# The first two tiles behind a norm, multiplied before the norm's row is known

## Chip, cores and metric

One core of one Trainium2 chip runs the whole program. The metric is the device time of one execution in microseconds (us), less is better.

## What is computed

The reference is a model of 512 tokens of width 1024: a first block of two layers (each an FFN, a token mix of attentions, another FFN), a final norm, and a later block with four branches and one last FFN. What the change touches is the norm in front of two products:

```python
def rms_norm(x):
    xf = x.astype(jnp.float32)
    return (xf * lax.rsqrt(jnp.mean(xf * xf, -1, keepdims=True) + NORM_EPS)).astype(x.dtype)
...
    h = rms_norm_2(x, norm1_g)          # later block
    z = h @ w_in + b_in
...
    h2 = rms_norm_2(x, norm2_g)         # last FFN
    x = x + jnp.square(jax.nn.relu(h2 @ w_up)) @ w_down
```

The norm of a token is one number per token; the gain is one number per feature. The kernel keeps x transposed (features on partitions, tokens along the free axis), so a token's number stands in a row that is the same on all partitions, and multiplies a product's columns alike whether it is applied before or after the matmul.

## The kernel before

All of x (eight pieces of 128 features by 512 tokens) stays on chip. Each matrix product is made of output tiles of 128 features: eight pieces k, and for each three matmuls (lines 445 to 447), because both operands are split into a high and a low part (`uh` and `ul` for the activations, `wh` and `wl` for the weights). A tile has so 24 matmuls of 128x512.

Weights come in the order of one list, `plan()`. SyncE loads a tile into one of five `raw` buffers; ScalarE rounds it into one of three `wh` buffers (line 943), VectorE takes the remainder (line 1427, `wl`); both do this when their own program reaches `get` for the tile two before it, and ScalarE then waits until TensorE is done with the tile three before it. `fm` handles one tile, `fm_pair` two tiles piece by piece, so that pieces can be used as they are made. ScalarE and VectorE evict the results. Each engine's order is the order of its own function, written out by hand, with semaphores between them.

Results go to eight banks in a ring: `take` gives the next one and waits until what was in it has been evicted (a "free" signal). At line 689 the counter of the ring is set to 4, `second()` makes the ring six banks long from bank 0 on, and its end makes it eight again from bank 0 on.

In front of the later block (stage "s") and of the last FFN (stage "up") the order is: TensorE sums the squares (line 488; passes with one column, against a column of ones), VectorE makes means, GpSimd the power -1/2 (line 2095), VectorE diagonal matrices (line 1465), TensorE turns them into a row on all partitions (line 495), then `apply` for each k: VectorE multiplies x by gain and row (line 1498), ScalarE copies this into `uh` (line 977), VectorE takes the remainder into `ul` (line 1461), and only then TensorE multiplies piece k. In front of the later block there are two norms in a row, the final one and the block's own; their rows are made together, and `final(k)` (ScalarE, line 1228) and GpSimd (line 2166) bring x itself up to date during the first tiles. The last down tiles of stage f21 and the tiles of `wo2`, which stand ahead of the two seams, end with an update of x (lines 1517, 1515); GpSimd and ScalarE square it as it comes.

Behind the row ScalarE evicts the later block's first tiles into `lqk` (line 1237); in the last FFN it applies Relu (line 1004), VectorE squares (line 1538), ScalarE rounds into `fh` (line 1010) and VectorE makes `fl`.

Of the kernel before, what the change touches and what calls it, by code (L numbers as in the profile page):

```python
# [14 lines left out]
def plan():  # L15
# [14 lines left out]
    def ffn(g, u, d, nf, ahead=False):  # L30
        for a, n in chunks(nf, CHUNK_FF):
            for j in range(a, a + n):
                if ahead and j < 4:
                    continue
                if j == 0 and u:
                    pair(g, 0, u, 0)
                elif j < 2 and not u:
                    if j == 0:
                        pair(g, 0, g, 1)
# [66 lines left out]
    for c in range(2, 13):  # L106
        fm("zml", 8, c)
# [136 lines left out]
def program(nc, A, OUT):  # L244
# [66 lines left out]
    with ExitStack() as c:  # L311
# [6 lines left out]
        with ExitStack() as d:  # L318
            lqk = sb(d, "lqk", [128, 8, 512])
# [80 lines left out]
    bank_of = {}  # L400
# [12 lines left out]
    def tensor_engine(pe, TE):  # L413
# [55 lines left out]

        def tm(g, name, nk, w, per, h, l, key):  # L470
# [20 lines left out]
        def row(g, dg):  # L491
# [4 lines left out]
            ins.then_inc(*s_pe.up(("ps", g)))  # L496

# [7 lines left out]
        def ffn(st, first=False):  # L505
# [190 lines left out]


# [213 lines left out]
        o = take(("fs", 0))  # L911
        pe.wait_ge(*s_pool["sq", "s"])
        sums(o, 0, acc)
        pe.wait_ge(*s_pool["sq fin"])
        sums(o, 4, more).then_inc(*s_pe.up(("ps", ("fs", 0))))
        o = take(("fs", 1))
        pe.wait_ge(*s_act["tail", "s"])
        sums(o, 0, tmp[1]).then_inc(*s_pe.up(("ps", ("fs", 1))))
        o = take(("fs", 2))
        pe.wait_ge(*s_act["tail fin"])  # L920
        sums(o, 0, tmp[3]).then_inc(*s_pe.up(("ps", ("fs", 2))))
        row(("r1",), tmp[2])
        row(("r", "s"), tmp[0])
        second()
        norm("up", tail("up"), tmp[2])
# [3 lines left out]
    def scalar_engine(act, SC):  # L929
# [36 lines left out]

        def copy(g, dst, src, key, scale=1.0):
# [17 lines left out]

        def norm(st):
# [3 lines left out]
        def ffn(st, after, first=False):  # L990
            _, g, u, d, nf = stages[st]
            tiles.side = list(ADA.get(st, []))
            for a0, n in chunks(nf, CHUNK_FF):
                for j in range(n):
                    jj = a0 + j
                    s = tmp[jj % 4]
                    if jj == 0 and not first:
                        fm_pair(g, 0, u or g, 0 if u else 1)
                    elif (u or jj > 1) and not (first and jj < 4):
# [11 lines left out]
                for m in range(8):  # L1011
                    fm(d, n, m, a0, st)
                    if a0 + n == nf and st == "f21":
# [3 lines left out]
                        elif m < 7:  # L1017
                            if m > 2:
                                act.wait_ge(*s_pool["fin", m - 2])
                            SC.activation(tmp[2 + m % 2][:], x[:, m, :], ACT.Square, scale=col("fin", m)).then_inc(*s_act.up(("fin", m)))  # L1020
            if after:
                square(after, 7, tmp[1])
            if st == "f21":
                act.wait_ge(*s_pool["fin", 5])
                SC.activation(tmp[3][:], x[:, 7, :], ACT.Square, scale=col("fin", 7)).then_inc(*s_act.up("tail fin"))
            while tiles.side:
# [203 lines left out]
        def second():  # L1230
            act.wait_ge(*s_dve["bgh"])
            fm_pair("zml", 0, "zml", 1)
            for i in range(8):
                if i > 1:
# [15 lines left out]
            tokens("zmlT")  # L1250
            c = Clock(0)
# [124 lines left out]
            for m in range(8):  # L1376
                fm("wo2", 8, m)
            square("up", 7, tmp[1])
            barrier("s")
# [35 lines left out]
    def vector_engine(dve, V):  # L1415
# [42 lines left out]

        def low(dst, src, hi, wait, key):
# [23 lines left out]
        def apply(st, key, src, n, g, dst_h, dst_l, scale, shift=None, before_k=None, after_k=None):  # L1483
# [7 lines left out]
            for k in range(n + 1):  # L1491
                if k < n:
# [3 lines left out]
                    if after_k and k:  # L1496
                        dve.wait_ge(*s_act["row", st])
                    V.scalar_tensor_tensor(tmp[k % 4][:], src[:, k, :], scale(k), more[:] if after_k and k else bank(g)[:], MUL, MUL).then_inc(
                        *s_dve.up(("ap", st, k), frees=g if k == (0 if after_k else n - 1) else None))
# [19 lines left out]
        def ffn(st, after, first=False):  # L1519
            _, g, u, d, nf = stages[st]  # L1520
            tiles.side = list(ADA.get(st, []))
            for a0, n in chunks(nf, CHUNK_FF):
                for j in range(n):
                    jj = a0 + j
                    s = tmp[jj % 4]
                    if jj == 0 and not first:
                        fm_pair(g, 0, u or g, 0 if u else 1)
                    elif (u or jj > 1) and not (first and jj < 4):
# [7 lines left out]
                    else:  # L1536
                        dve.wait_ge(*s_act["gate", st, jj])
                        V.tensor_tensor(s[:], s[:], s[:], MUL).then_inc(*s_dve.up(("prod", st, jj)))
                    low(fl[:, j, :], s[:], fh[:, j, :], s_act["hh", st, jj], ("h", st, jj))
                for m in range(8):  # L1540
                    fm(d, n, m, a0, st)
                    gate = mod[:, MOD[st] + 16 + m:MOD[st] + 17 + m] if st in MOD else None
                    update(("d", st, a0, m), m, gate, ("x", after if a0 + n == nf else (st, a0), m))
            while tiles.side:
# [273 lines left out]
        def second():  # L1818
            u = ("u", "s")
            V.tensor_scalar(bgh[:], col("bg", 0, 32), 0.5, None, MUL).then_inc(*s_dve.up("bgh"))  # L1820
            fm_pair("zml", 0, "zml", 1)
            for i in range(2, 9):
# [202 lines left out]
            for m in range(8):  # L2025
                fm("wo2", 8, m)
                dve.wait_ge(*s_pool["fx", m])
                update(("wo", "s", m), m, None, ("x", "up", m))
            barrier("s")
# [24 lines left out]
        for l in range(2):  # L2054
# [8 lines left out]
            modulated(f"f2{l}")  # L2063
            ffn(f"f2{l}", "f11" if l == 0 else "s")
# [10 lines left out]
        V.tensor_tensor(small[:, 64:72], col("fin", 0, 8), col("n1", 0, 8), MUL).then_inc(*s_dve.up("fn"))  # L2075
# [6 lines left out]
        apply("s", ("u", "s"), x, 8, ("r", "s"), uh, ul, lambda k: small[:, 64 + k:65 + k])  # L2082
        second()
        norm("up", 2, tmp[2])
        apply("up", ("u", "up"), x, 8, ("r", "up"), uh, ul, lambda k: col("n2", k))
# [368 lines left out]
```

## Time and profile before

| what | value |
|---|---|
| median of 3 runs | 3535.2 us (3529.13 to 3535.67) |
| the profiled execution's own time | 3529.9 us |
| its span, first to last instruction | 3528.0 us |
| TensorE busy | 3436.2 us |
| mean granted clock of TensorE | 0.982 |

Times in the rows below count from the start of the span. A duration of a matmul is longer than the distance between two of them, since they are pipelined. The granted clock is a share of full speed: 1.00 is 2.4 GHz, 0.50 is 1.2 GHz.

### The profile page before, as it was taken

To read this page: it belongs to the slowest core of one execution; us is meant where nothing else is said; L and a number is where in the kernel's file an instruction comes from. 1 tells how busy PE (TensorE), PEld (TensorE's weight loads), DVE (VectorE), ACT (ScalarE), POOL (GpSimd) and SP (SyncE) were. 2 spreads that over 40 slices of the span, in tenths; PEclk is the share of its full clock that TensorE was granted. 3 is DMA by queue.
4 is the path that set the end of the run, shared out by engine and by line. 5 is a ranking of instruction groups with operands and counts; after the bars stand their busy time and mean duration, and the time that the engine had idled before them with its cause. 6 is when DMAs were issued, how large, how long until landed. Compare 5 with 4: busy or idle time off the path is not lost.

```text
span 3528.0 us, 40785 instructions
## 1 busy us (share of the span) xinstructions
PE 3436.2 (97%) x16646; PEld 2758.8 (78%) x16646; DVE 1771.6 (50%) x3082; ACT 1177.8 (33%) x1974; POOL 269.8 (8%) x226
## 2 busy tenths in 40 slices
PE   8999999999999999999999999999999999999999
PEld 6888786777888788887777878887788777878887
DVE  7666446565666633334655643334453655454433
ACT  3222236542222232223555232223321444223322
POOL 0000210002000200021100200012011000120000
PEclk9999999999999999999999999999999999999999
DMA  6555322123565533233210322322221223122232
GB/s 236 204 210 190 106 81 69 43 73 112 188 223 188 177 98 99 92 99 101 71 49 28 112 84 87 104 84 94 63 76 54 75 78 115 45 93 84 97 107 78
DMA packets 120218, 376.37 MB, mean 107 GB/s; under 512 B 13280, under 2 KB 28000, under 8 KB 120032
## 3 DMA queue, kind: packets, MB, share of 16 engines
q1 hardware_dynamic: 120032, 373.76, 32.0%
q8 instruction: 133, 2.18, 0.2%
q14 instruction: 53, 0.43, 0.0%
HBM read 371.61 MB, written 2.10 MB: 106 GB/s over the span
## 4 chain that ended last, share of the span: by engine, by line
PE 92%; DVE 4%; ACT 2%; issue 1%; POOL 1%; DMA 0%; SPq 0%; POOLq 0%; ACTq 0%; DVEq 0%
PE ps L445 26%; PE ps L447 26%; PE ps L446 26%; PE ps L659 2%; PE ps L682 2%; PE ps L554 2%; PE ps L488 1%; PE ps L495 1%; PE ps L479 1%; PE ps L481 1%; PE ps L480 1%; DVE s_wl L1427 1%; ACT s_wh L943 1%; POOL s_small L2095 0%; PE ps L521 0%
## 5 line engine op out<-in xcount | busy, mean ns | idle before, releaser
L445 PE MATMUL ps<-s_uh,s_wh 128*128 128x512 f32 x2824 | 1137.6, 403 | 32.4 <-DVE s_ul L1489 12.8
L1427 DVE TENSOR_TENSOR s_wl<-s_raw,s_wh 128x1024 fp32r<-128x1024 f32 (+3 forms) x645 | 705.3, 1094 | 859.6 <-ACT s_wh L943 858.1
L447 PE MATMUL ps<-s_ul,s_wh 128*128 128x512 f32 x2824 | 1111.3, 394 | 0.0
L446 PE MATMUL ps<-s_uh,s_wl 128*128 128x512 f32 x2824 | 1110.9, 393 | 0.0
L943 ACT ACTIVATE s_wh<-s_raw 128x1024 fp32r<-128x1024 f32 (+3 forms) x645 | 588.2, 913 | 743.2 <-PE ps L447 545.2
L445 PEld LDWEIGHTS ps<-s_uh,s_wh 128*128 128x128 f32 x2824 | 537.4, 190 | 175.8 <-issue 49.4
L447 PEld LDWEIGHTS ps<-s_ul,s_wh 128*128 128x128 f32 x2824 | 536.5, 190 | 115.1
L446 PEld LDWEIGHTS ps<-s_uh,s_wl 128*128 128x128 f32 x2824 | 538.0, 191 | 109.4 <-issue 2.4
L447 PE MATMUL ps<-s_fl,s_wh 128*128 128x512 f32 x960 | 378.2, 394 | 0.0
L445 PE MATMUL ps<-s_fh,s_wh 128*128 128x512 f32 x960 | 378.2, 394 | 0.0
L446 PE MATMUL ps<-s_fh,s_wl 128*128 128x512 f32 x960 | 378.2, 394 | 0.0
L445 PEld LDWEIGHTS ps<-s_fh,s_wh 128*128 128x128 f32 x960 | 179.5, 187 | 44.4
L447 PEld LDWEIGHTS ps<-s_fl,s_wh 128*128 128x128 f32 x960 | 179.5, 187 | 44.4
L446 PEld LDWEIGHTS ps<-s_fh,s_wl 128*128 128x128 f32 x960 | 179.5, 187 | 44.4
L1010 ACT ACTIVATE s_fh<-s_tmp 128x512 fp32r<-128x512 f32 x120 | 75.8, 632 | 407.3 <-DVE s_tmp L1535 382.4
L1004 ACT ACTIVATE s_tmp<-ps 128x512 f32<-128x512 f32 x120 | 71.7, 598 | 354.7 <-PE ps L447 350.4
L1436 DVE CUSTOM_DVE_ANT_0 s_raw<-s_raw,s_crow 128x1024 f32<-128x1024 f32 x144 | 181.3, 1259 | 0.8 <-DMA s_raw<-w 0.8
L1535 DVE TENSOR_TENSOR s_tmp<-s_tmp,ps 128x512 f32<-128x512 f32 x88 | 60.5, 687 | 179.5 <-PE ps L447 175.8
L2101 POOL TENSOR_TENSOR s_acc<-s_x 128x512 f32<-128x512 f32 x7 | 7.8, 1110 | 1608.7 <-DVE s_x L1517 1546.3
L1461 DVE TENSOR_TENSOR s_fl<-s_tmp,s_fh 128x512 fp32r<-128x512 f32 x120 | 83.1, 692 | 83.7 <-ACT s_fh L1010 83.7
L1517 DVE SCALAR_TENSOR_TENSOR s_x<-ps,s_mod,s_x 128x512 f32<-128x512 f32 x80 | 60.0, 750 | 99.1 <-PE ps L447 99.1
L1126 ACT ACTIVATE s_mT<-ps 128x128 f32<-128x128 f32 (+3 forms) x144 | 57.3, 431 | 145.4 <-PE ps L554 145.4
(400 smaller groups left out, 3336.5 us busy)
## 6 DMA issues: line engine op xcount, KB each, us to landing
s_raw<-w SPq DMA_DIRECT2D x616, 512.0 KB, 3.6
s_raw<-w SPq DMA_DIRECT2D x96, 192.0 KB, 2.4
s_raw<-w SPq DMA_DIRECT2D x64, 256.0 KB, 2.6
s_raw<-w SPq DMA_DIRECT2D x19, 128.0 KB, 2.0
s_x<-x SPq DMA_DIRECT2D x4, 512.0 KB, 7.1
out<-s_x SPq DMA_DIRECT2D x8, 256.0 KB, 2.1
s_raw<-w SPq DMA_DIRECT2D x4, 420.0 KB, 3.7
s_crow<-crow SPq DMA_DIRECT2D x2, 512.0 KB, 3.5
```

Of the source, the lines that this page charges most:

```text
L445: TE.matmul(o, w_hi(i, k), h, start=first, stop=False)
L446: TE.matmul(o, w_lo(i, k), h, start=False, stop=False)
L447: return TE.matmul(o, w_hi(i, k), l, start=False, stop=last)
L554: ins = TE.transpose(o[:, sl(j)], p[:, sl(j)], ident)
L659: TE.matmul(o[g][:, 0:L], q, k, start=True, stop=True).then_inc(*s_pe.up(("ps", ("S", (st, 2 * t + g)))))
L682: ins = TE.matmul(o[g], v, mT[(n + g) % 4][:, sl(j)], start=kind == "mla" and j == 0, stop=j == i and (kind == "mla" or br == 1))
L943: SC.activation(wh[slot[t]][:, 0:n], raw[t % NRAW][:, 0:n], ACT.Copy).then_inc(*s_hi.up(("hi", t)))
L1004: SC.activation(s[:], bank(("g", st, jj))[:], ACT.Silu if u else ACT.Relu).then_inc(*s_act.up(("gate", st, jj), frees=("g", st, jj)))
L1010: SC.activation(fh[:, j, :], s[:], ACT.Copy).then_inc(*s_act.up(("hh", st, jj)))
L1427: V.tensor_tensor(wl[w][:, 0:n], raw[t % NRAW][:, 0:n], wh[w][:, 0:n].bitcast(F32), SUB).then_inc(*s_lo.up(("lo", t)))
L1436: V.tensor_tensor_reduce(raw[i % NRAW][:], raw[i % NRAW][:], crow[:], 1.0, 0.0, MUL, ADD, mod[:, o:o + 1]).then_inc(*s_dve.up(("raw", i)))
L1461: V.tensor_tensor(dst, src, hi.bitcast(F32), SUB).then_inc(*s_dve.up(key))
```

## The change

For stages "s" and "up" a second pair of arrays, `gxh` and `gxl`, holds x times the gain only, made piece by piece while the stage before updates x (`gained`). The first two output tiles are multiplied from it (`raw_pair`); the sums and the row are made on TensorE between its pieces (`between`: before k = 2 and k = 6 in stage "s", before k = 2 and k = 4 in "up"). Their evictions multiply by the row. `uh` and `ul` are made as before, but during and after the raw pair, and are first used by tiles 2 and 3, which are now a pair. Halfway in `apply`, at k = 4, ScalarE and VectorE run the four `get` calls of tiles 0 to 3 (`two_pairs`), which split tiles 2, 3 and 4. In stage "s" the eviction of the two raw tiles is a copy into `lqk`, a product on VectorE and a bias on ScalarE; in "up" it is a product between Relu and square, in `acc` and `more`. The ring of six in `second()` starts at a bank computed from the row's.

```diff
+        def raw_pair(st, g0, g1, name, between):
+            i0, i1 = get(name, 0, 0), get(name, 0, 128)
+            o0, o1 = take(g0), take(g1)
+            for k in range(8):
+                between.get(k, lambda: None)()
+                pe.wait_ge(*s_dve["gx", st, k])
+                a = three(o0[:, :], i0, k, gxh[:, k, :], gxl[:, k, :], k == 0, k == 7)
+                b = three(o1[:, :], i1, k, gxh[:, k, :], gxl[:, k, :], k == 0, k == 7)
+            a.then_inc(*s_pe.up(("w", i0), ("ps", g0)))
+            b.then_inc(*s_pe.up(("w", i1), ("ps", g1)))
...
# TensorE, ffn
-                    if jj == 0:
-                        fm_pair(("g", st, 0), g, 0, ("u", st, 0) if u else ("g", st, 1), u or g, 0 if u else 1, ("u", st))
-                    elif u or jj > 1:
+                    if jj == 0 and not u:
+                        raw_pair(st, ("g", st, 0), ("g", st, 1), g, {2: lambda: norm_sums(st, tail(st)), 4: lambda: row(("r", st), tmp[2])})
+                    elif jj == 0:
+                        fm_pair(("g", st, 0), g, 0, ("u", st, 0), u, 0, ("u", st))
+                    elif jj == 2 and not u:
+                        fm_pair(("g", st, 2), g, 2, ("g", st, 3), g, 3, ("u", st))
+                    elif u or jj > 3:
...
# TensorE, second; final_sums and final_rows hold what stood ahead of second() before
-            ring[:] = [list(range(6)), 0]
+            raw_pair("s", ("ml", 0), ("ml", 1), "zml", {2: final_sums, 6: final_rows})
+            ring[:] = [list(range(6)), (bank_of["r", "s"] + 1) % 8 % 6]
             pe.wait_ge(*SEL)
-            fm_pair(("ml", 0), "zml", 0, ("ml", 1), "zml", 1, u)
-            for i in range(2, 13):
+            fm_pair(("ml", 2), "zml", 2, ("ml", 3), "zml", 3, u)
+            for i in range(4, 13):
...
# ScalarE and VectorE: a hook in apply
+        def two_pairs(name):
+            def at(k):
+                if k == 4:
+                    fm_pair(name, 0, name, 1)
+                    fm_pair(name, 2, name, 3)
+            return at
...
# ScalarE, in the last down tiles of f21 and in the tiles of wo2, and once behind each loop
+        def gained(st, m, gain):
+            SC.activation(gxh[:, m, :], x[:, m, :], ACT.Identity, bias=0.0, scale=gain(m)).then_inc(*s_act.up(("gx", st, m)))
...
# VectorE, after update(m - 1), and for 6 and 7 after update(7)
+        def gained(st, m, gain):
+            dve.wait_ge(*s_act["gx", st, m])
+            V.scalar_tensor_tensor(gxl[:, m, :], x[:, m, :], gain(m), gxh[:, m, :].bitcast(F32), MUL, SUB).then_inc(*s_dve.up(("gx", st, m)))
...
# ScalarE, second
-            act.wait_ge(*s_dve["bgh"])
-            fm_pair("zml", 0, "zml", 1)
-            for i in range(8):
-                if i > 1:
+            for i in range(2):
+                copy(("ml", i), lqk[:, i, :], bank(("ml", i))[:], ("ml raw", i))
+            for i in range(2):
+                act.wait_ge(*s_dve["ml", i])
+                SC.activation(lqk[:, i, :], lqk[:, i, :], ACT.Identity, bias=col("bml", i)).then_inc(*s_act.up(("lqk", i)))
+            for i in range(2, 8):
+                if i > 3:
                     fm("zml", 8, i)
...
# ScalarE, the calls
-        apply("s", 8, uh)
+        apply("s", 8, uh, None, two_pairs("zml"))
         copy(("r1",), acc[:], bank(("r1",))[:], "rowcopy")
         second()
-        apply("up", 8, uh)
+        apply("up", 8, uh, None, two_pairs("up2"))
...
# VectorE, ffn
                         dve.wait_ge(*s_act["gate", st, jj])
+                        if jj < 2:
+                            V.tensor_tensor(s[:], s[:], bank(("r", st))[:], MUL).then_inc(*s_dve.up(("normed", st, jj), frees=("r", st) if jj else None))
+                            dve.wait_ge(*s_dve["normed", st, jj])
...
# VectorE, behind apply("s")
+        for i in range(2):
+            dve.wait_ge(*s_act["ml raw", i])
+            V.tensor_tensor(lqk[:, i, :], lqk[:, i, :], bank(("r", "s"))[:], MUL).then_inc(*s_dve.up(("ml", i), frees=("r", "s") if i else None))
```

## Rows read from the trace of the kernel before

**Rows 1.** The page: span, TensorE's share, and the chain by line.
```profile
span 3528.0 us, 40785 instructions
...
PE 3436.2 (97%) x16646; PEld 2758.8 (78%) x16646; DVE 1771.6 (50%) x3082; ACT 1177.8 (33%) x1974; POOL 269.8 (8%) x226
...
PE ps L445 26%; PE ps L447 26%; PE ps L446 26%; PE ps L659 2%; PE ps L682 2%; PE ps L554 2%; PE ps L488 1%; PE ps L495 1%; PE ps L479 1%; PE ps L481 1%; PE ps L480 1%; DVE s_wl L1427 1%; ACT s_wh L943 1%; POOL s_small L2095 0%; PE ps L521 0%
```

**Rows 2.** Timeline of TensorE, seam before the later block: start us, duration us, work.
```profile
2403.64 0.95 PE L488 MATMUL ps<-s_cst,s_acc 128*128 128x1 f32 x8
...
2411.24 3.75 PE L495 MATMUL ps<-s_tmp,s_cst 128*128 128x128 f32 x16 [2.40 <-DVE s_tmp L1465]
2417.40 0.76 PE L445 MATMUL ps<-s_uh,s_wh 128*128 128x512 f32 x1 [2.40 <-DVE s_ul L1461]
```

**Rows 3.** The same of TensorE at the seam before the last FFN.
```profile
3159.10 0.95 PE L488 MATMUL ps<-s_cst,s_acc 128*128 128x1 f32 x8
...
3163.58 2.04 PE L495 MATMUL ps<-s_tmp,s_cst 128*128 128x128 f32 x8 [1.77 <-DVE s_tmp L1465]
3168.03 0.76 PE L445 MATMUL ps<-s_uh,s_wh 128*128 128x512 f32 x1 [2.40 <-DVE s_ul L1461]
```

**Rows 4.** Windows: length, five engines' busy us, granted clock, DMA share, GB/s.
```profile
2417.40:2422.90 5.50, 5.50 (x13) 4.34 (x14) 5.50 (x10) 2.53 (x4) 0.00 (x0) 0.50 0.01 3
...
2584.48:2590.20 5.72, 5.72 (x15) 4.46 (x16) 2.68 (x9) 0.00 (x0) 4.21 (x4) 0.50 0.26 78
...
3119.20:3122.60 3.40, 3.40 (x10) 2.63 (x9) 3.13 (x3) 1.06 (x1) 1.04 (x1) 0.51 0.44 151
...
3161.00:3163.50 2.50, 0.82 (x8) 0.73 (x7) 0.42 (x3) 0.00 (x0) 1.02 (x1) 1.00 0.00 0
...
3168.00:3173.90 5.90, 5.87 (x14) 4.64 (x15) 5.90 (x10) 2.81 (x5) 0.00 (x0) 0.50 0.01 3
```

**Rows 5.** Timeline of VectorE, seam before the later block and its first tiles.
```profile
2402.89 1.23 DVE L1427 TENSOR_TENSOR s_wl<-s_raw,s_wh 128x1024 fp32r<-128x1024 f32 x1 [2.43 <-ACT s_wh L943]
...
2408.88 0.16 DVE L1474 SCALAR_TENSOR_TENSOR s_small<-ps,s_small 128x4 f32<-128x4 f32 x1 [1.54 <-PE ps L488]
...
2412.19 0.88 DVE L1465 TENSOR_SCALAR s_tmp<-s_cst,s_small 128x128 f32<-128x128 f32 x4
...
2419.69 0.74 DVE L1498 SCALAR_TENSOR_TENSOR s_tmp<-s_x,s_small,ps 128x512 f32<-128x512 f32 x1
...
2439.52 2.18 DVE L1427 TENSOR_TENSOR s_wl<-s_raw,s_wh 128x1024 fp32r<-128x1024 f32 x1 [4.30 <-ACT s_wh L943]
```

**Rows 6.** Timeline of ScalarE: the last copy, the row copy, then evictions.
```profile
2424.24 0.63 ACT L977 ACTIVATE s_uh<-s_tmp 128x512 fp32r<-128x512 f32 x1 [0.63 <-DVE s_tmp L1498]
2424.78 0.58 ACT L969 ACTIVATE s_acc<-ps 128x512 f32<-128x512 f32 x1
...
2447.50 0.69 ACT L1237 ACTIVATE s_lqk<-ps,s_cst 128x512 f32<-128x512 f32 x1 [2.58 <-PE ps L447]
2448.09 1.32 ACT L1228 ACTIVATE s_x<-s_x,s_cst 128x512 f32<-128x512 f32 x2
...
2452.94 0.69 ACT L1237 ACTIVATE s_lqk<-ps,s_cst 128x512 f32<-128x512 f32 x1 [2.58 <-PE ps L447]
```

**Rows 7.** Timeline of ScalarE in the last FFN.
```profile
3182.63 0.63 ACT L1010 ACTIVATE s_fh<-s_tmp 128x512 fp32r<-128x512 f32 x1 [0.76 <-DVE s_tmp L1538]
...
3184.62 0.63 ACT L1010 ACTIVATE s_fh<-s_tmp 128x512 fp32r<-128x512 f32 x1 [0.87 <-DVE s_tmp L1538]
...
3198.74 0.60 ACT L1004 ACTIVATE s_tmp<-ps 128x512 f32<-128x512 f32 x1 [2.50 <-PE ps L447]
```

**Rows 8.** Timeline of TensorE at two places elsewhere in the later block.
```profile
2580.46 4.16 PE L488 MATMUL ps<-s_cst,s_lqk 128*128 128x1 f32 x32
...
3118.58 0.50 PE L445 MATMUL ps<-s_uh,s_wh 128*128 128x512 f32 x1 [1.81 <-DVE s_ul L1461]
```

**Rows 9.** Timeline of GpSimd in the later block's first tiles.
```profile
2438.06 2.55 POOL L2166 TENSOR_TENSOR s_x<-s_x,s_acc 128x512 f32<-128x512 f32 x2 [26.10 <-ACT s_x L1228]
```

More of the change, by code:

```diff
@@ L36, in ffn @@
                     pair(g, 0, u, 0)
-                elif j < 2 and not u:
-                    if j == 0:
-                        pair(g, 0, g, 1)
+                elif j < 4 and not u:
+                    if j % 2 == 0:
+                        pair(g, j, g, j + 1)
                 else:
@@ L105, in plan @@
     pair("zml", 0, "zml", 1)
-    for c in range(2, 13):
+    pair("zml", 2, "zml", 3)
+    for c in range(4, 13):
         fm("zml", 8, c)
@@ L496, in row, with norm_sums @@
             ins.then_inc(*s_pe.up(("ps", g)))
+        def norm_sums(st, parts):
+            for j, (ap, wait) in enumerate(parts):
+                o = take(("ms", st, j))
+                pe.wait_ge(*wait)
+                sums(o, 0, ap).then_inc(*s_pe.up(("ps", ("ms", st, j))))
         def norm(st, parts, dg):
@@ L695, in mix, with final_sums, final_rows @@
             s_pe.mark(("end", st))
+        def final_sums():
+            o = take(("fs", 0))
+            pe.wait_ge(*s_pool["sq", "s"])
+            sums(o, 0, acc)
+            pe.wait_ge(*s_pool["sq fin"])
+            sums(o, 4, more).then_inc(*s_pe.up(("ps", ("fs", 0))))
+            o = take(("fs", 1))
+            pe.wait_ge(*s_act["tail", "s"])
+            sums(o, 0, tmp[1]).then_inc(*s_pe.up(("ps", ("fs", 1))))
+            o = take(("fs", 2))
+            pe.wait_ge(*s_act["tail fin"])
+            sums(o, 0, tmp[3]).then_inc(*s_pe.up(("ps", ("fs", 2))))
+        def final_rows():
+            row(("r1",), tmp[2])
+            row(("r", "s"), tmp[0])
         def gate(c, b):
@@ L995, in ffn @@
                     jj = a0 + j
[L996 to L999, printed above, removed]
+                    s = tmp[jj % 4] if u or jj > 1 else (acc, more)[jj]
+                    if jj == 0 and u and not first:
+                        fm_pair(g, 0, u, 0)
+                    elif (u or jj > 3) and not (first and jj < 4):
                         fm(g, 8, jj, 0, st)
@@ L1250, in second @@
             tokens("zmlT")
+            act.wait_ge(*s_dve["bgh"])
             c = Clock(0)
@@ L1457, in tm, with two_pairs, at @@
                 get(name, k0, 0)
+        def two_pairs(name):
+            def at(k):
+                if k == 4:
+                    fm_pair(name, 0, name, 1)
+                    fm_pair(name, 2, name, 3)
+            return at
         def low(dst, src, hi, wait, key):
@@ L1524, in ffn @@
                     jj = a0 + j
[L1525 to L1528, printed above, removed]
+                    s = tmp[jj % 4] if u or jj > 1 else (acc, more)[jj]
+                    if jj == 0 and u and not first:
+                        fm_pair(g, 0, u, 0)
+                    elif (u or jj > 3) and not (first and jj < 4):
                         fm(g, 8, jj, 0, st)
@@ L1543, in ffn @@
                     update(("d", st, a0, m), m, gate, ("x", after if a0 + n == nf else (st, a0), m))
+                    if st == "f21" and a0 + n == nf:
+                        for k in (m - 1,) if m < 7 else (6, 7):
+                            if k >= 0:
+                                gained("s", k, lambda k: small[:, 64 + k:65 + k])
             while tiles.side:
@@ L1820, in second @@
             V.tensor_scalar(bgh[:], col("bg", 0, 32), 0.5, None, MUL).then_inc(*s_dve.up("bgh"))
-            fm_pair("zml", 0, "zml", 1)
-            for i in range(2, 9):
+            for i in range(4, 9):
                 fm("zml", 8, i)
```

39 lines of the change are left out of this document (20 added, 19 removed).

## Prediction

> **What bounds the kernel now.** I read the page first: TensorE is busy 97% of the span, and three of its lines (445 to 447), 26% each, are 78% of the chain that ended last [rows 1]. So only time in which TensorE stands still or runs at its lower clock can be won. Then I read TensorE's timeline at the two places that the diff touches. At the seam before the later block the dense matmuls end at 2403.64 us; sums, rows and two waits of 2.40 us follow, and the next dense matmul starts at 2417.40, a hole of 13.8 us [rows 2]. At the seam before the last FFN the hole is 3159.10 to 3168.03, 8.9 us [rows 3]. Then the windows: after each hole the granted clock is 0.50 for 5.5 and 5.9 us, in which 13 matmuls take 5.5 us, 0.42 each, where a tile of 24 takes 5.44 at full clock, 0.227 each [rows 4, 6]; such a stretch costs 2.6 us. A seam thus costs its hole and 2.6 us, and some of it (sums and rows on TensorE) must be done anyway. Last I read VectorE and ScalarE [rows 5 to 7], because what the change puts into the hole still has to be released by them in their program order.
>
> **The change part by part.** All absolute times are those of the profiled execution.
>
> *Added ahead of the seams.* Eight ScalarE copies with a gain (0.6 to 0.7 us, like the copies of [rows 6]) and eight VectorE remainders (0.7 us) per seam. They lie in loops where TensorE works 7.7 us (f21's down tiles) or 5.44 us (wo2's) a turn and VectorE is busy under half of it; I cost them at nothing. The tile nearest to trouble is zml's first: its split moves 0.6 us and is still done about 2.5 us before use. If that cover were gone it would cost its 0.6 us. Line 1427 for zml's second tile ends at 2404.12 [rows 5], so the raw pair starts at 2404.2. The last two remainders wait for the update behind it (0.75), a square, another square and the last copy: about 2407.5, long before k = 6 wants them.
>
> *Later block, TensorE.* k = 0, 1 of the pair: 12 matmuls x 0.227 = 2.7, to 2406.9. Then `final_sums`, 32 passes in a row. The nearest row is 32 such passes in 4.0 us (2580.46 to 2584.48), and behind them 5.7 us at clock 0.50 [rows 4, 8]. I take 3.8 (the x8 of [rows 2] takes 0.95), to 2410.7. k = 2 to 5: 24 x 0.227 = 5.4, plus the lower clock: nothing to 2.6, I take 2.1 as the row that it is nearest to shows it; to 2418.2. The diagonals come 4.2 us after the last sum (before: 2408.88 to 2413.07, [rows 5]), at 2415, so they no longer hold TensorE. Two rows at 0.9: the norm's row is there at R = 2420.0 (before: 2415.0). k = 6, 7: to 2422.7.
>
> *Later block, the wait that nobody removed.* The next pair (zml 2, 3) takes two banks. The bank ring: line 689 sets the counter to 4, then mix takes 24, the norm 3, f21 22 + 22 + 16: 91, which is bank 3 of 8. So ml 0 gets bank 3, ml 1 bank 4, the sums 5, 6, 7, the rows 0 and 1. `(1 + 1) % 8 % 6` starts the ring of six at 2: ml 2 gets bank 2, **ml 3 gets bank 3, which still holds ml 0**. `fm_pair` takes both banks before its first matmul, and `take` waits for the eviction of ml 0. That eviction is a ScalarE copy that stands in program order behind all eight copies of `apply("s")`, the three weight splits of `two_pairs` and the row copy. Before, the eighth copy starts 9.2 us after the row (2424.24 - 2415.0) and the row copy ends at +10.4 [rows 6]. `two_pairs` at k = 4 puts three rounds of line 943 (1.0 each) and three of line 1427 (1.1 to 1.2) between remainder 2 and product 4: the splits end at R + 9.2 instead of product 4 starting at +4.7 (2419.69, [rows 5]), so all later steps are 4.5 later. Row copy ends R + 14.9, ml 0 copy R + 15.5. TensorE restarts at 2435.5, after 12.8 us of standing still. (Queued behind this wait on TensorE is everything; on ScalarE and VectorE nothing waits for TensorE till then, so it is no deadlock.) By the Trainium skill ("TensorE: Matmul & The Clock Gate", section "Architectural detail") ScalarE and VectorE are strict FIFO: by that rule the copy cannot slip ahead though its matmuls end at 2422.7. Could it, TensorE would wait only for zml's tile 3 and restart at R + 8.2; [rows 6] show the row copy behind the eighth copy though its own matmuls were done 10 us before, so the rule and the trace agree.
>
> *Later block, after it.* The pair is 48 x 0.227 = 10.9, and after so long a hole 2.6 for the clock [rows 4]: E = 2449.0. Now ScalarE has two tiles to evict at once, with four finals behind them, before it may split zml 5, because `fm` for i = 2, 3 is gone: 2 x (0.7 + 1.3) = 4.0 [rows 6] and 1.05 for line 943. The remainder then runs beside GpSimd's row product and takes 2.18 as at 2439.52, not the 1.23 it takes alone [rows 5, 9]: tile 5 is ready at E + 7.3, wanted at E + 5.44, a stall of 1.9 (1.0 if GpSimd doesn't disturb). By the Trainium skill ("SBUF — State Buffer", section "SBUF: two separate sides") VectorE and GpSimd hold a shared port pair as an exclusive lock for a whole instruction; by that the remainder might start up to one GpSimd instruction late, which gives the same stall within 0.3. Tile 5 is evicted at 2449.0 + 7.3 + 5.4 + 0.2 = 2461.9. Before: 2452.9 [rows 6]. **The block loses 9.0 us**; with the clock kept through the sums and the stall of 1.0 it loses 6 to 7, with the clock lost once more behind the 1.9 stall 10.5.
>
> *Last FFN.* The ring restarts at 0: the raw pair has banks 0 and 1, the sums 2 and 3, the row 4, the next pair 5 and 6, so no such wait. Both tiles are split before 3159.1. k = 0, 1: 2.7; 16 passes 1.7 (0.95 for eight, overlapping, [rows 3]); k = 2, 3: 2.7, in which the 2.3 us of mean, GpSimd and diagonals are hidden; row 0.9: R = 3167.15. k = 4 to 7: 5.4, to 3172.6. The split of up2's third following tile ends at R + 8.2 = 3175.3 (same hook): a stall of 2.7. Pair to E = 3186.2. Then the evictions: two tiles with one VectorE product more each (0.7; with its wait 2.7 us a tile instead of 2.0, [rows 7]) end at R + 19.7, and tiles 2 and 3 must be evicted before up2's tile 5 is split: relu, square, copy twice, 943, 1427: ready at R + 26.0 = 3193.1, wanted 3191.6. Before, tile 5 starts at 3198.6 (eviction of tile 4 at 3198.74, [rows 7]). That is 5.5 won. Against it stands the clock: behind a wait of 1.81 us at 3118.58 the granted clock was 0.51 for 3.4 us [rows 4, 8], so the stall of 2.7 probably costs half of such a stretch, partly hidden by the VectorE chain (0.8), and the sums or the second stall the rest. **I take 4.0 won**, bounds 2.2 and 5.5.
>
> **Sum.** 9.0 - 4.0 = 5.0 us more, bounds 1.3 and 8.3. The profiled execution took 3529.9 (span 3528.0), so 3534.9 by it. The three runs have 3529.1, 3535.2 and 3535.7; against their median it would be 3540.2. I name 3538, between.
>
> **The rivals.**
> 1. *Slower past what can be told.* The same mechanism, with the clock lost behind the stalls at both seams: later block 10.5, FFN only 2.2 won or a little less: +8 to +9, 3542. For it speaks that a 1.8 us wait was enough once; against, that in the last seam the clock was still 1.00 up to 3163.5, 4.4 us after the dense matmuls [rows 3, 4].
> 2. *Faster: the bank wait decides nothing.* If ml 0 were evicted early (my bank count or the order on ScalarE wrong), TensorE restarts at R + 8.2, and if the clock also holds through the sums, R = 2417.8, E = 2436.9, tile 5 evicted at 2449.8: 3.1 won, with the FFN's 5.5 it is -8.6: 3527. It turns faster as soon as the restart is earlier than about R + 10. Against it stand the counted banks.
> 3. *The seams close altogether.* TensorE finds work all through: both holes less sums and rows, 11 + 9 us, 3515. Against it: the split of the third tile needs the weight buffer that the raw pair frees, and stands behind four copies.
> 4. *It does nothing measurable for another reason*, both seams smaller than I think: it falls into my forecast's case.
>
> **Numbers.** A difference of 0.2% (7 us) is about what can be told from none here. Forecast (+1 to +7): 0.60. Rival 1: 0.27. Rival 2: 0.08, half of it within 0.2%. Rival 3: 0.03. Rival 4: 0.02. So faster 0.08, same 0.64, slower 0.28. Range: the bounds +1.3 and +8.3 on both anchors, widened by the runs' own spread: 3529 to 3547; the forecast's own is 3531 to 3543.
>
> **What would show it.** In the profile after: the raw pair starting at 2404 us without the 13.8 us hole; then TensorE waiting some 13 us for a ScalarE copy into s_lqk, the first thing to look for; clock 0.5 after it; a stall of 1 to 2 us for line 1427 one tile after the second pair. At the last seam a wait of 2.7 us for line 1427's counterpart and one of 1 to 2. The prediction is wrong if that copy comes right after its matmuls, if the remainders before the seams delay the tiles of f21 or wo2, or if the four products before the hook take far longer than theirs before.

## The result and the profile after

| what | before | changed |
|---|---|---|
| median | 3529.99 us (3521.75 to 3535.67, 20 runs) | 3537.01 us (3530.05 to 3552.87, 20 runs) |
| profiled execution's own time | 3529.91 us | 3533.86 us |
| its span | 3528.0 us | 3532.0 us |
| TensorE busy | 3436.2 us | 3432.2 us |
| mean granted clock | 0.982 | 0.984 |

The ratio of the times is 1.0025, with a 95% interval of 1.0015 to 1.0035. The medians are 7.0 us apart, which is 0.2%: the change brought nothing, and lost a little, just at the edge of what can be told. The forecast was 5.0 us more. The profiled executions differ by 4.0 us, and thirteen of the twenty timed ones lie between 3530 and 3538 us; the other seven lie between 3541 and 3553, which the forecast did not have.

TensorE's busy time fell by 4 us and the span grew by 4 us. The waits of TensorE say where it stood still; the columns are: us in total, times, longest.

```profile
PE ps L448 <- ACT s_lqk L1006: 12.9, 1, 12.9
...
PE ps L448 <- DVE s_wl L1479: 6.9, 9, 2.8
```

The first is the wait that the prediction told the reader to look for first. TensorE's timeline at the seam before the later block, to be read beside [rows 2], shows its place: start, duration, work, and in brackets the idle time and who ended it.

```profile
2401.95 0.48 PE L448 MATMUL ps<-s_gxh,s_wh 128*128 128x512 f32 x1 [0.41 <-DVE s_wl L1479]
...
2404.80 0.95 PE L503 MATMUL ps<-s_cst,s_acc 128*128 128x1 f32 x8
2405.60 1.03 PE L503 MATMUL ps<-s_cst,s_more 128*128 128x1 f32 x8
...
2413.88 1.95 PE L510 MATMUL ps<-s_tmp,s_cst 128*128 128x128 f32 x16
2415.58 0.48 PE L448 MATMUL ps<-s_gxh,s_wh 128*128 128x512 f32 x1
...
2431.51 0.76 PE L448 MATMUL ps<-s_uh,s_wh 128*128 128x512 f32 x1 [12.91 <-ACT s_lqk L1006]
...
2451.18 0.50 PE L448 MATMUL ps<-s_uh,s_wh 128*128 128x512 f32 x1 [0.30 <-DVE s_wl L1479]
```

The hole of 13.8 us is gone: from 2401.95 on TensorE has work, sums and rows lie between matmuls of `gxh`, and it never waits for them. Then, with the raw pair done, it stands still for 12.91 us. ScalarE's timeline shows what it stands for (this answers to [rows 6]).

```profile
2420.57 2.93 ACT L972 ACTIVATE s_wh<-s_raw 128x1024 fp32r<-128x1024 f32 x3
2425.83 0.63 ACT L1014 ACTIVATE s_uh<-s_tmp 128x512 fp32r<-128x512 f32 x1 [2.33 <-DVE s_tmp L1562]
...
2429.62 0.63 ACT L1014 ACTIVATE s_uh<-s_tmp 128x512 fp32r<-128x512 f32 x1 [0.63 <-DVE s_tmp L1562]
2430.15 0.58 ACT L1006 ACTIVATE s_acc<-ps 128x512 f32<-128x512 f32 x1
2430.63 1.08 ACT L1006 ACTIVATE s_lqk<-ps 128x512 f32<-128x512 f32 x2
...
2444.79 0.69 ACT L1284 ACTIVATE s_lqk<-ps,s_cst 128x512 f32<-128x512 f32 x1 [11.48 <-PE ps L450]
...
2456.99 0.69 ACT L1284 ACTIVATE s_lqk<-ps,s_cst 128x512 f32<-128x512 f32 x1 [3.21 <-PE ps L450]
```

The three weight splits, four copies and the row copy all come before the two copies into `lqk` at 2430.63 (lines 1014 and 1006 are the changed kernel's 977 and 969). The first of these two ends about 2431.2, and TensorE starts at 2431.51. VectorE says when the row was there, and how long its part of the splits takes (this answers to [rows 5]).

```profile
2415.86 1.41 DVE L1562 SCALAR_TENSOR_TENSOR s_tmp<-s_x,s_small,ps 128x512 f32<-128x512 f32 x2 [3.25 <-PE ps L510]
...
2421.64 3.50 DVE L1479 TENSOR_TENSOR s_wl<-s_raw,s_wh 128x1024 fp32r<-128x1024 f32 x3 [1.04 <-ACT s_wh L972]
```

The windows give the clock (length, busy us of the five engines, granted clock, DMA share, GB/s), as [rows 4] did.

```profile
2404.80:2408.40 3.60, 3.60 (x34) 3.60 (x33) 0.78 (x4) 0.00 (x0) 0.00 (x0) 1.00 0.00 1
2408.40:2415.80 7.40, 7.40 (x42) 6.40 (x42) 2.48 (x13) 0.00 (x0) 2.03 (x2) 1.00 0.01 2
2423.80:2437.40 13.60, 5.89 (x14) 4.67 (x15) 8.45 (x14) 5.32 (x9) 0.00 (x0) 0.50 0.33 116
3184.90:3188.30 3.40, 3.40 (x10) 2.65 (x9) 3.40 (x7) 1.34 (x3) 0.00 (x0) 0.50 0.94 276
```

Here the clock stayed at 1.00 through the sums and the pieces behind them, and was 0.50 from within the long wait until 5.9 us behind its end. The seam before the last FFN, answering to [rows 3], shows on TensorE and then on ScalarE:

```profile
3167.26 0.47 PE L448 MATMUL ps<-s_gxh,s_wh 128*128 128x512 f32 x1 [0.88 <-DVE s_x L1579]
...
3170.09 0.94 PE L503 MATMUL ps<-s_cst,s_acc 128*128 128x1 f32 x8
...
3174.64 1.05 PE L510 MATMUL ps<-s_tmp,s_cst 128*128 128x128 f32 x8
...
3183.98 0.47 PE L448 MATMUL ps<-s_uh,s_wh 128*128 128x512 f32 x1 [2.77 <-DVE s_wl L1479]
...
3202.43 0.47 PE L448 MATMUL ps<-s_uh,s_wh 128*128 128x512 f32 x1 [0.25 <-DVE s_wl L1479]
```

```profile
3208.19 0.60 ACT L1044 ACTIVATE s_tmp<-ps 128x512 f32<-128x512 f32 x1 [2.55 <-PE ps L450]
```

**Where the 4.0 us went.** I follow four stretches, from the end of the dense matmuls to the eviction of tile 5 at either seam, and what lies around them. The end of the dense matmuls is taken as the start of the last one plus the usual distance of 0.23 us: 2401.37 and 3166.22 in the changed kernel, 2403.64 and 3159.10 before. (The idle time that the profile gives in brackets counts from the modelled end of the last matmul, about 0.16 us later.) Tile 5's evictions start at 2456.99 and 3208.19 in the changed kernel, at 2452.94 and 3204.18 before.

| stretch | before | changed | difference |
|---|---|---|---|
| start to the end of f21's dense matmuls | 2403.64 | 2401.37 | -2.3 |
| to the eviction of tile 5 in the later block | 49.30 | 55.62 | **+6.3** |
| from there to the end of wo2's matmuls | 706.16 | 709.23 | +3.1 |
| to the eviction of tile 5 in the last FFN | 45.08 | 41.97 | **-3.1** |

The work of the first and third rows is not the change's, and they differ by stretches of lower clock that come and go between executions. In the third it lies in one place, shown by this window of the changed kernel and, under it, the one of the same stage before. A clock of 0.80 over 25 us is 10.0 us at 0.50, one of 0.93 is 3.5; the 6.5 us more at half the clock cost 3.2 us.

```profile
3045.00:3070.00 25.00, 25.00 (x128) 21.46 (x127) 8.13 (x23) 3.87 (x5) 8.09 (x8) 0.80 0.07 22
...
3041.00:3066.00 25.00, 25.00 (x144) 21.57 (x142) 8.80 (x24) 3.87 (x5) 9.15 (x8) 0.93 0.09 22
```

What the change itself did at its two seams is +6.3 - 3.1 = +3.2 us.

Two more profiles of the changed kernel (runs 7 and 11) have the later block at 55.8 us, +6.5, though in them the clock did fall behind the sums. It then came back sooner behind the long wait, so that the block is hardly longer:

```profile
2408.90:2412.40 3.50, 3.50 (x10) 2.75 (x9) 1.88 (x11) 0.00 (x0) 2.03 (x2) 0.52 0.02 5
```

(Run 7.) The loss of 6.3 to 6.5 us at this seam thus stands in three profiles.

### The profile page after: what moved, and what is told of

It is laid out like the page before. It is cut to its first block, busy times and chain, and to the rows that moved or that the text cites. A ratio compares the mean times of both kernels' runs of the same rounds, so it can differ in the third digit from the quotient of the medians.

```text
span 3532.0 us, 40829 instructions
## 1 busy us (share of the span) xinstructions
PE 3432.2 (97%) x16646; PEld 2753.4 (78%) x16646; DVE 1788.3 (51%) x3102; ACT 1188.0 (34%) x1992; POOL 271.8 (8%) x226
## 3 DMA queue, kind: packets, MB, share of 16 engines
q8 instruction: 133, 2.18, 0.2%
## 4 chain that ended last, share of the span: by engine, by line
PE 91%; DVE 4%; ACT 3%; issue 1%; DMA 0%; POOL 0%; SPq 0%; ACTq 0%; POOLq 0%; DVEq 0%
PE ps L448 26%; PE ps L449 25%; PE ps L450 25%; PE ps L684 2%; PE ps L707 2%; PE ps L579 2%; PE ps L503 1%; DVE s_wl L1479 1%; PE ps L494 1%; PE ps L496 1%; PE ps L495 1%; PE ps L510 1%; ACT s_wh L972 1%; PE ps L542 0%; POOL s_small L2173 0%
## 5 line engine op out<-in xcount | busy, mean ns | idle before, releaser
L448 PE MATMUL ps<-s_uh,s_wh 128*128 128x512 f32 x2792 | 1124.7, 403 | 43.7 <-ACT s_lqk L1006 12.9
L449 PE MATMUL ps<-s_uh,s_wl 128*128 128x512 f32 x2792 | 1098.8, 394 | 0.0
L450 PE MATMUL ps<-s_ul,s_wh 128*128 128x512 f32 x2792 | 1098.7, 394 | 0.0
```

Of the source, the lines that this page charges most:

```text
L448: TE.matmul(o, w_hi(i, k), h, start=first, stop=False)
L449: TE.matmul(o, w_lo(i, k), h, start=False, stop=False)
L450: return TE.matmul(o, w_hi(i, k), l, start=False, stop=last)
```

## The experiments

The seven edited kernels compute the whole of the reference; runs 7, 8, 10 and 11 repeat kernels. Runs 1 to 4 shared a chip, whose kernel before had a median of 3528.58 us (3521.91 to 3535.5, 29 runs); runs 5 to 8 another one, 3530.04 (3520.19 to 3536.03, 16 runs); runs 9 to 11 a third, 3529.21 (3522.84 to 3542.69, 26 runs).

**1. Other banks for the next pair.** Only the two tiles behind the raw pair change banks, to two that hold sums long since read.

```diff
             raw_pair("s", ("ml", 0), ("ml", 1), "zml", {2: final_sums, 6: final_rows})
-            ring[:] = [list(range(6)), (bank_of["r", "s"] + 1) % 8 % 6]
+            ring[:] = [[2, 5], 0]
             pe.wait_ge(*SEL)
             fm_pair(("ml", 2), "zml", 2, ("ml", 3), "zml", 3, u)
+            ring[:] = [list(range(6)), 4]
```

> The changed kernel, but tiles 2 and 3 of the later block's first product go to banks 2 and 5, which are free, instead of 2 and 3; from tile 4 on the banks are as before. Theory (bank): the 12.9 us wait of TensorE for the ScalarE copy into s_lqk goes away, and the next thing that is late is the split of tile 3 (line 1479), so the restart comes 7.3 us earlier (row end + 8.2 instead of + 15.6); with less or no time at the low clock behind it the whole is 7 to 9 us shorter than the changed kernel, a little shorter than the kernel before. Rival (the hook): ScalarE and VectorE are what is late anyway, tile 5 waits for them all the same; then the restart is earlier but the end is no more than 2 us earlier.

Measured: median 3524.21 us (3520.46 to 3544.25, 11 runs), ratio 1.0001 (0.9987 to 1.0015); the profiled execution 3520.46. The median is 4.4 us below that of the kernel before, but the interval of the ratio can't tell it from no difference. The wait for `s_lqk` is gone, and another stands in its place:

```profile
2421.19 0.77 PE L448 MATMUL ps<-s_uh,s_wh 128*128 128x512 f32 x1 [5.67 <-DVE s_wl L1480]
```

The row came at 2412.80, so TensorE restarts 8.4 us behind it instead of 15.7, and from the dense end (2398.32) to tile 5's eviction (2445.39) it is 47.1 us, against 55.6 in the changed kernel and 49.3 before. The wait for the bank is the cause of the loss: without it this seam is 8.5 us shorter, and in this profile 2.2 us shorter than before. That win isn't safe. This execution kept the full clock behind the sums; run 4, with the same code at this seam, did not and took 50.5 us, 1.2 more than before. Two of the eleven runs took 3541 and 3544 us.

**2 and 3. One seam alone.** The other seam's part is undone in full, with its `gained` calls, its `raw_pair` and its hook.

```diff
# 2, later block as before
-            raw_pair("s", ("ml", 0), ("ml", 1), "zml", {2: final_sums, 6: final_rows})
+            final_sums()
+            final_rows()
...
-        apply("s", 8, uh, None, two_pairs("zml"))
+        apply("s", 8, uh)
# 3, last FFN as before
-                        raw_pair(st, ("g", st, 0), ("g", st, 1), g, {2: lambda: norm_sums(st, tail(st)), 4: lambda: row(("r", st), tmp[2])})
+                        fm_pair(("g", st, 0), g, 0, ("g", st, 1), g, 1, ("u", st))
...
-        apply("up", 8, uh, None, two_pairs("up2"))
+        apply("up", 8, uh)
```

> The changed kernel with the later block's part undone: only the last FFN multiplies its first two tiles without the row. Theory: 3 us faster than the kernel before (this seam from the last dense matmul to the eviction of tile 5: 41.9 us in the profile after, 45.1 before), and no execution far above the others. Rival (the two parts hang together, or the slow tail of the changed kernel's times, 3542 to 3553, belongs to this part): no gain, or such a tail.

> The changed kernel with the last FFN's part undone: only the later block multiplies its first two tiles without the row. Theory: 6 us slower than the kernel before (55.4 us from the last dense matmul to the eviction of tile 5 after, 49.3 before), with the 12.9 us wait for s_lqk in its profile; the tail of slow executions is here, if it comes from that long wait. Rival: under 3 us slower, and no tail.

Measured: with the last FFN's part alone 3527.03 us (3521.2 to 3534.01, 12 runs), ratio 0.9993 (0.9985 to 1.0002), and in its profile the seam is 3.1 us shorter; the timing can't tell 3 us from none. With the later block's part alone 3543.23 us (3537.28 to 3554.6, 6 runs), ratio 1.0043 (1.0028 to 1.0058); in its profile the wait for `s_lqk` is 12.9 us again and the block takes 56.1 us, 6.8 more than before, but the median is 15 us up. The loss is the later block's, and part of it is not at the seam (runs 7 and 8).

**4. Both rings.** Run 1, and the last FFN's ring starts at bank 2, so that its raw pair doesn't take bank 1 from wo2's last tile.

```diff
             s_pe.mark(("end", "s"))
-            ring[:] = [list(range(8)), 0]
+            ring[:] = [list(range(8)), 2]
```

> As e1, and the bank ring of the last FFN starts at 2 instead of 0, so that its raw pair no longer takes bank 1, which holds wo2's last tile. Theory: the 0.9 us wait for s_x (line 1579) at the start of the raw pair goes away, and the time is 1 us shorter than e1. Rival: TensorE then waits 0.9 us later on, at the sums or the row, and the time is that of e1.

Measured: 3523.93 us (3519.68 to 3544.01, 11 runs), ratio 0.9996 (0.9982 to 1.001). By the timings it can't be told from run 1. In the last FFN the wait of 0.88 us is gone, and the wait at tile 5 has grown from 0.25 to 1.34 us:

```profile
3188.30 0.47 PE L448 MATMUL ps<-s_uh,s_wh 128*128 128x512 f32 x1 [1.34 <-DVE s_wl L1480]
```

From the dense end (3153.74) to tile 5's eviction (3194.02) it is 40.3 us, against 41.97 in the changed kernel: 1.7 less. Of this 1.0 is the bank: the raw pair starts at the dense end, and in the changed kernel 1.04 us behind it. The other 0.7 goes with the clock: the two tiles behind the wait of 2.77 us ran at 1.00 here, and at 0.50 for 3.4 us in the changed kernel's profile.

```profile
3170.30:3173.90 3.60, 3.51 (x16) 2.95 (x17) 3.60 (x6) 1.16 (x2) 0.00 (x0) 1.00 0.85 291
```

Some 1.0 of the 1.7 us that such a stretch costs TensorE is hidden by VectorE's chain, which is why the wait at tile 5 is longer where the clock is full. The lower clock goes with the bank wait in every profile on record: all six with the wait of 0.88 us ahead of the raw pair (the changed kernel, runs 1, 2, 5, 7 and 11) have 3.4 us at 0.50 behind the wait of 2.77, and all four without it (runs 4, 6 and 10, and run 9, whose later wait is 1.83) have 1.00. So the whole difference between the two profiles may be the bank's; that the one wait brings the lower clock behind the other is not shown. At the other seam this execution had the lower clock behind the sums that the prediction had allowed for:

```profile
2404.50:2411.30 6.80, 6.80 (x24) 5.93 (x24) 2.62 (x15) 0.00 (x0) 2.03 (x2) 0.50 0.01 2
```

**5. The banks as changed, but evicted earlier.** ScalarE's two copies move from behind `apply` to its k = 4, ahead of the three weight splits. The banks stay those of the changed kernel; only the copies' place in ScalarE's order changes.

```diff
+        def evict_then_split(k):
+            if k == 4:
+                for i in range(2):
+                    copy(("ml", i), lqk[:, i, :], bank(("ml", i))[:], ("ml raw", i))
+            pairs_at(k)
...
-        apply("s", 8, uh, None, two_pairs("zml"))
+        apply("s", 8, uh, None, evict_then_split)
```

> The changed kernel with its banks as they are, but ScalarE evicts the later block's two raw tiles at k = 4 of apply, ahead of the three weight splits, instead of behind apply. Theory (the eviction is late because of its place in ScalarE's order): bank 3 comes free 1 us earlier than the splits, TensorE waits for line 1479 instead, and restarts 9.3 us behind the row (after: 15.65, with the bank exchanged: 8.4). Rival (a wait for more than the bank, such as for lqk's other uses): the restart stays at 15 us.

Measured: 3527.97 us (3522.3 to 3532.32, 10 runs), ratio 0.9991 (0.9982 to 1.0001). TensorE waits 6.59 us, now for the split, restarts 9.3 us behind the row, as expected, and the block takes 49.5 us, within 0.2 us of what it took before:

```profile
2424.80 1.06 ACT L1006 ACTIVATE s_lqk<-ps 128x512 f32<-128x512 f32 x2
2425.75 2.95 ACT L972 ACTIVATE s_wh<-s_raw 128x1024 fp32r<-128x1024 f32 x3
```

So the loss needs both, the shared bank and the copy's late place in ScalarE's order: with the copies ahead of the three splits and the last four copies of `apply`, 6.1 of the 6.3 us are back. The two copies now stand ahead of the splits and hold them up, so that TensorE restarts 0.9 us later than in run 1 (9.3 against 8.4). What is left is the wait for the split, and run 6 asks whether that too is a matter of place.

**6. The splits moved ahead too.** From run 4: zml's third tile is split ahead of `apply`, its fourth at k = 2, its fifth behind `apply`; the four calls of `final` pairs move two tiles later.

```diff
+        def in_three(name):
+            def at(k):
+                if k == 0:
+                    get(name, 0, 0)
+                    get(name, 0, 128, 1)
+                if k == 2:
+                    get(name, 0, 256, 1)
+            return at
...
-                for k in {2: (0, 1), 3: (2, 3), 4: (4, 5), 5: (6, 7)}.get(i, ()):
+                for k in {4: (0, 1), 5: (2, 3), 6: (4, 5), 7: (6, 7)}.get(i, ()):
...
-        apply("s", 8, uh, None, two_pairs("zml"))
+        apply("s", 8, uh, None, in_three("zml"))
+        get("zml", 0, 384, 1)
```

> As e4, and in the later block the split of tile 2 stands ahead of apply, that of tile 3 at k = 2 and that of tile 4 behind apply, instead of all three at k = 4; the finals of x follow tiles 4 to 7 instead of 2 to 5, so that tile 5's split is not queued behind them. Theory: after the raw pair only tile 3's split is on the path; TensorE restarts 5.2 us behind the row (e1: 8.4), the stall of 0.4 us at tile 5 goes, and the time is 3 us below e4. Rival: pieces k = 2 and on come later now, because the split stands ahead of them, and TensorE waits in the pair for line 1554's counterpart of this stage what it won before.

Measured: 3520.25 us (3518.35 to 3524.66, 6 runs), ratio 0.9974 (0.9961 to 0.9987); again as run 10: 3519.77 us (3515.37 to 3534.46, 9 runs), ratio 0.9975 (0.9963 to 0.9986).

```profile
2400.00 0.47 PE L448 MATMUL ps<-s_gxh,s_wh 128*128 128x512 f32 x1 [0.42 <-DVE s_wl L1491]
...
2420.26 0.47 PE L448 MATMUL ps<-s_uh,s_wh 128*128 128x512 f32 x1 [1.98 <-DVE s_wl L1491]
```

The wait is down to 1.98 us, the one at tile 5 is gone, and the dense end to tile 5's eviction takes 44.5 us (2399.42 to 2443.91): 4.8 less than before, 11.1 less than the change. The profiles of runs 9 and 10 have 44.5 too.

**7 and 8. Again the changed kernel, and run 3's.** One execution each, to catch one of the long ones in a profile.

> The changed kernel once more, to see where the time of its slow executions lies (some took 3546 to 3553 us, most 3532 to 3538). If this one is slow, the theory that they lose it to the granted clock wants more time at 0.50 in it than the 114 us of the profile after, by twice the difference in time; the rival, that an engine other than TensorE is longer, wants a longer wait in it.

> The kernel of e3 once more, for the same reason: its executions are spread from 3537 to 3555 us. If this one is slow: more time at 0.50 than in the profile of e3 (124 us), or a longer wait.

Measured: 3532.61 us for the changed kernel, no long one; 3554.69 us for run 3's, 17.4 us over its first profile, with the same waits (12.9 us for `s_lqk` in both) and a mean granted clock of 0.976 against 0.983. Most of the difference is one stretch of lower clock, in a branch of the later block some 600 us behind the seam:

```profile
3034.90:3072.40 37.50, 37.50 (x130) 30.15 (x129) 4.68 (x6) 5.55 (x8) 4.04 (x4) 0.50 0.03 8
```

The same place in the profile of run 3, where the clock was back after one short stretch:

```profile
3031.40:3034.80 3.40, 3.40 (x13) 2.69 (x11) 2.18 (x3) 2.12 (x3) 0.00 (x0) 0.50 0.03 5
3034.90:3054.00 19.10, 19.10 (x115) 15.60 (x114) 1.83 (x3) 3.33 (x5) 2.44 (x3) 1.00 0.05 15
```

TensorE is busy all through both. What the stretch costs is read by setting VectorE's instructions of the two profiles beside each other, one by one: up to 3026 us run 8 is 3.8 us late, nearly all of it from ahead of the seam, and from 3078 us on 17.4. So the stretch, less what run 3 has of lower clock at the same place (3.4 us, and 6.8 more from 3058.7 on), makes 13.6 of the 17.4 us. The profile of run 10 (execution of 3534.5 us) has the same stretch, that of run 6 (the same kernel, 3519.2 us) has not; between these two the same reading gives 13.5 us:

```profile
3019.40:3056.90 37.50, 37.50 (x130) 30.12 (x127) 4.75 (x6) 5.55 (x8) 4.04 (x4) 0.50 0.03 8
```

```profile
3019.40:3035.20 15.80, 15.80 (x101) 12.82 (x99) 2.89 (x4) 1.96 (x3) 0.00 (x0) 1.00 0.06 17
```

**9 and 11. The last FFN too, and the changed kernel beside it.** From run 6: up2's third tile is split ahead of `apply`, its fourth at k = 4, its fifth behind it, and the one after is fetched ahead of an eviction. Run 11 is the changed kernel again.

```diff
-                if k == 2:
+                if k == (2 if name == "zml" else 4):
                     get(name, 0, 256, 1)
...
+                    elif not u and jj == 3:
+                        fm(g, 8, 4, 0, st)
...
-        apply("up", 8, uh, None, two_pairs("up2"))
+        apply("up", 8, uh, None, in_three("up2"))
+        get("up2", 0, 384, 1)
```

> As e6, and the same in the last FFN: the split of up2's tile 2 ahead of apply, that of tile 3 at k = 4, that of tile 4 behind apply, and the splits of tiles 5 and 6 ahead of the eviction of tile 3 instead of behind it. Theory: the wait of 2.77 us behind the raw pair becomes 2.4 (tile 3's buffer is free only when the raw pair ends), the 1.3 us wait at tile 5 goes; 1.6 us less than e6, within what can be told only by the profile. Rival: ScalarE's evictions set the pace here, and a wait of over 1 us appears at tile 6 or 7.

> The kernel of e6 again, timed beside e9 and the changed kernel on one chip. Theory: 0.26% shorter than the kernel before, as in e6, and none of its executions over 3540 us. Rival: its few executions in e6 happened to have no slow one, and with more of them the tail of e1 and e4 (3540 to 3544 us) shows and takes the gain.

> The changed kernel again, beside these two on the same chip. Theory: 4 to 9 us above the kernel before (profiles 4, medians 7), 12 to 17 above e6. Rival: on this chip, no difference from the kernel before.

Measured: run 9 3517.72 us (3509.75 to 3534.86, 12 runs), ratio 0.9973 (0.9958 to 0.9989); run 11 3534.1 us (3531.01 to 3547.25, 12 runs), ratio 1.0013 (1.0002 to 1.0025). In run 9's profile the wait behind the last FFN's raw pair is 1.83 us instead of 2.77, and the one at tile 5 is gone:

```profile
3170.16 0.47 PE L448 MATMUL ps<-s_uh,s_wh 128*128 128x512 f32 x1 [1.83 <-DVE s_wl L1494]
```

By median it is 2 us under run 10, by ratio the two can't be told apart. Both are 14 to 16 us under the changed kernel on the same chip, and run 11 puts the changed kernel 4.9 us above the kernel before. They are the only two orders tried that beat the kernel before clear of the noise. The expectation of run 10, no execution over 3540 us, held in number only: its one long execution (3534.5) has the stretch of run 8, and three of run 9's twelve lie at 3531 to 3535 us.

## Why the prediction was right, step by step

- **Ahead of the seams, nothing: right.** The raw pair starts 0.58 us behind the dense end, forecast 0.56. The eight copies and remainders delay no tile of f21.
- **The sums: 3.5 us** (2404.80 to 2408.28), forecast 3.8. **The clock behind them was mis-sized** in this profile: the sum had 2.1 us for it, and the window from 2408.40 on shows 1.00. Of the eleven profiles whose kernel has the raw pair here, nine have the lower clock behind the sums: eight 3.4 us, a loss of 1.7, and run 4 6.8 us, a loss of 3.4, over the bound of 2.6. The changed kernel's first profile and run 1's paid nothing. Where it came, the stretch behind the long wait was shorter: the two together cost 2.9 to 3.4 us in the five profiles with that wait, where the sum had 2.1 + 2.6 = 4.7.
- **The bank wait: right in mechanism and size**, 12.91 us against 12.8, the restart 15.7 us behind the row against 15.5. Run 1 removes it by other banks and run 5 by an earlier copy, so it is shown twice, and rival 2, that it decides nothing, is out. Run 1 also gives that rival's own number, a restart at the row plus 8.4 against 8.2. Its claim that the block turns faster below plus 10 does not hold by itself: at 9.3 (run 5) it was even with before, at 8.4 it won 2.2 us in run 1 and lost 1.2 in run 4, where the clock had made the row itself later.
- **After it**, the second pair takes 13.8 us from the restart, forecast 13.5 (tile 5 starts at 2451.18, 0.46 us later than the pace of 0.227 gives; taken back by that and by tile 4's 5.44 the pair ends at 2445.28). **The second term too large** is the stall at tile 5: those 0.46 us in place of 1.9, a start at E + 5.9 and not E + 7.3. I had ScalarE begin the two evictions at E; it began the first at 2444.79, 0.5 before it, and was at the split at E + 3.1 instead of 4.0, and the remainder that tile 5 needs, the first of two that take 3.87 us together, was done within 1.7 us, where I had 2.18. By the Trainium skill ("SBUF — State Buffer", section "SBUF: two separate sides") the VectorE instruction would wait for a whole GpSimd one. The profile after gives 1.77 us for such a remainder at 2453.81, longer than the 1.23 it takes alone and shorter than the 2.18 of [rows 5]; a remainder is slowed beside GpSimd by amounts that differ, and no run here separates a lock from shared bandwidth.
- **The block: +6.3 us, forecast 9.0.** Of the 2.7 missing, 2.1 is the clock in the sums and 1.4 the stall; the other steps took back 0.8. The text gave 6 to 7 for just this case. It would have been 9 by the text with the clock lost in the sums, and runs 7 and 11 show 6.5 there: adding a full stretch of lower clock behind the wait to the one behind the sums was too much.
- **The last FFN: -3.1 us, forecast -4.0.** The wait for the split is 2.77 us, forecast 2.7. **The step that was wrong is the banks**: "so no such wait". There is a small one, 0.88 us: the ring restarts at 0, wo2's last tile still has bank 1, and the raw pair takes both banks before its first matmul, so it stands until that tile's update. I counted the banks behind the raw pair and not those ahead of it; run 4 shows that it cost 1.0, and perhaps the clock behind the next wait as well. The 5.5 us of work was 4.8 (45.08 less run 4's 40.3), and the clock behind the wait took 0.7 of it where I had 1.5.
- **The sum: +3.2 us by the seams, +4.0 by the profiled executions, +4.9 and +7.0 by the medians of the two timings**, forecast +5.0. Luck helped: the block's loss was forecast 2.7 us too large and the last FFN's gain 0.9 too large, which partly cancel; and 3538, named between two anchors, lies so near the median of 3537 because of long executions that the sum knew nothing of (the median before came out at 3530, to which +5 gives 3535). The lower bound of +1.3 isn't what its own terms give: 9.0 less 2.1 and 0.9 is 6.0, less 5.5 it is +0.5. Rival 1, 8 to 9 us, fails by its mechanism: in the block the clock was 1.00 on both sides of tile 5's start, and the last FFN won more than the 2.2 it was given. The first timing comes near its number all the same, for another reason.
- **What the prediction lacked** is the long stretch of lower clock behind the seam. It costs some 13.6 us when it comes, and it is seen in two profiled executions. How often it comes with which kernel is open: 7 of 20 executions of the changed kernel were over 3541 us in the first timing, 1 of 12 in run 11, and 4 of 6 of run 3's kernel; of the kernel before, none of the 65 in the first timing and beside runs 1 to 8 was over 3536.1, and 4 of the 26 beside runs 9 to 11 were at 3537.6 to 3542.7. The 12.9 us wait is not needed for it, since run 10's kernel hasn't got it. So what the first timing shows beyond the 4 us of the profiles is probably this, but that is argued from the spread, not shown.

## What to carry to other kernels

Work put into a hole only moves the wait to the next thing that is released late: list, for the first matmul behind the moved work, its operands **and** its output bank, and find the place of each releaser in its engine's program order. Here one copy that stood behind three splits and four copies ate the whole gain, and its place was worth 6 us (run 5); the splits' place, together with the exchanged banks, was worth 5 more (run 6). When a ring of banks is cut or restarted, count both the tile ahead and the tile behind.

## What the runs showed of the hardware

- In a branch made of small matmuls (64x64 and 128x128, with some of 128x512 between) TensorE's granted clock was 0.50 for 37.5 us with TensorE busy for all of them, and 1.00 in the same stage of the same kernel in another execution. In run 8 it was back at 3072.5 us, 5.3 us into a run of matmuls of 128x512. Between two such executions that makes 13.6 us, 0.4% of this kernel. The Trainium skill ("TensorE: Matmul & The Clock Gate", section "What's actually happening") lets the clock follow how busy the engine has been recently. Here it was busy 37.50 of 37.50 us by the profile and the clock stayed at 0.50, so the profile's busy time doesn't foretell it.
- Behind the same wait of 2.77 us in the last FFN the clock was 0.50 for 3.4 us in six profiles, all with a wait of 0.88 us some 14 us earlier, and 1.00 in three without that wait (runs 4, 6 and 10); behind run 9's 1.83 us it was 1.00 too. Whether the earlier wait brings it is not shown. Behind the 32 passes with one column it stayed at 1.00 in two profiles of eleven, was 0.50 for 3.4 us in eight and for 6.8 us in one. A term for the clock behind a short pause or such passes is thus a chance times 1.7 us or more, not a fixed cost.
